# Routed experts of a two-layer decoder block: one written-out run of weight tiles, tokens gathered in float32r, gates applied at the add

## The reference

```python
def moe_swiglu(h, w_router, w_gate, w_up, w_down):
    probs = jax.nn.softmax((h @ w_router).astype(jnp.float32), axis=-1)
    top_p, top_i = lax.top_k(probs, TOP_K)                       # TOP_K = 2, N_EXPERTS = 8
    top_p = top_p / jnp.sum(top_p, axis=-1, keepdims=True)
    gates = jnp.sum(jax.nn.one_hot(top_i, N_EXPERTS, dtype=jnp.float32) * top_p[..., None], axis=-2)
    y = jnp.zeros(h.shape, jnp.float32)
    for e in range(N_EXPERTS):
        y = y + gates[..., e:e + 1] * swiglu(h, w_gate[e], w_up[e], w_down[e]).astype(jnp.float32)
    return y.astype(h.dtype)
```

## Time and profile before

| | us |
|---|---|
| median of 3 runs | 1809.09 (1803.16 to 1809.59) |
| the profiled execution | 1802.93 |
| its span | 1801.2 |
| around the span | 1.7 |
| first matmul of an expert tile starts | 766.32 |
| last matmul of an expert tile starts | 1781.75 |
| output DMA is issued | 1796.81 |

### The profile page before, as it was taken

The page is one execution under the profiler, slowest core; times in us unless marked ns, Lnnn a source line. Parts: engine busy times, 40 slices in busy tenths (PEclk is TensorE's granted clock), DMA queues, the critical chain, the costliest instruction groups (busy, mean ns, idle before and its releaser), DMA issues.

```text
span 1801.2 us, 28357 instructions
## 1 busy us (share of the span) xinstructions
PE 1729.2 (96%) x11390; PEld 1442.9 (80%) x11390; DVE 1274.9 (71%) x1185; ACT 966.4 (54%) x977; POOL 31.3 (2%) x93
## 2 busy tenths in 40 slices
PE   7999899999899999799999999999999999999997
PEld 5756899999677997478878788888788887788785
DVE  4671545542477655688888789888788897888885
ACT  2351534432143223276767667767667676667673
POOL 5000000000100000000000000000000000000000
PEclk9997999999999999899999999999999999999998
DMA  9210255453232004179999899999899998999992
GB/s 325 77 46 0 93 165 186 166 185 122 93 120 94 3 5 176 49 281 365 351 356 362 300 361 361 345 347 359 305 354 353 363 343 332 329 365 353 356 357 107
DMA packets 191227, 432.81 MB, mean 240 GB/s; under 512 B 9907, under 2 KB 10931, under 8 KB 191092
## 3 DMA queue, kind: packets, MB, share of 16 engines
q1 hardware_dynamic: 190704, 430.76, 66.0%
q10 hardware_dynamic: 388, 0.14, 0.0%
HBM read 429.82 MB, written 1.05 MB: 239 GB/s over the span
## 4 chain that ended last, share of the span: by engine, by line
PE 84%; DVE 9%; ACT 4%; issue 3%; ACTq 0%; DVEq 0%
PE ps L1012 16%; PE ps L1014 15%; PE ps L1013 15%; PE ps L667 5%; PE ps L665 5%; PE ps L666 5%; PE ps L584 2%; PE ps L714 2%; PE ps L979 2%; PE ps L994 2%; DVE wsplit L1783 2%; PE ps L656 2%; PE ps L934 2%; PE ps L833 1%; PE ps L848 1%
## 5 line engine op out<-in xcount | busy, mean ns | idle before, releaser
L1783 DVE TENSOR_TENSOR wsplit<-raw_w,wsplit 128x2048 fp32r<-128x2048 f32 x336 | 750.0, 2287 | 68.4 <-ACT wsplit L1347 68.4
L1347 ACT ACTIVATE wsplit<-raw_w 128x2048 fp32r<-128x2048 f32 x336 | 624.2, 1914 | 63.6 <-PE ps L1014 63.6
L1012 PE MATMUL ps<-wsplit,xsplit 128*128 128x512 f32 x896 | 360.4, 402 | 9.6 <-DVE wsplit L1783 8.1
L1014 PE MATMUL ps<-wsplit,xsplit 128*128 128x512 f32 x896 | 350.7, 391 | 0.0
L1013 PE MATMUL ps<-wsplit,xsplit 128*128 128x512 f32 x896 | 350.2, 391 | 0.0
L1012 PEld LDWEIGHTS ps<-wsplit,xsplit 128*128 128x128 f32 x896 | 169.0, 189 | 47.7 <-DVE wsplit L1783 12.7
L1014 PEld LDWEIGHTS ps<-wsplit,xsplit 128*128 128x128 f32 x896 | 169.0, 189 | 36.6
L1013 PEld LDWEIGHTS ps<-wsplit,xsplit 128*128 128x128 f32 x896 | 169.3, 189 | 36.2 <-issue 3.1
L1012 PE MATMUL ps<-wsplit,hsplit 128*128 128x512 f32 x448 | 179.6, 401 | 0.0
L1014 PE MATMUL ps<-wsplit,hsplit 128*128 128x512 f32 x448 | 174.6, 390 | 0.0
L1013 PE MATMUL ps<-wsplit,hsplit 128*128 128x512 f32 x448 | 174.5, 389 | 0.0
(11 more groups left out here) (320 smaller groups left out, 2258.0 us busy)
## 6 DMA issues: line engine op xcount, KB each, us to landing
raw_w<-in_moe_w_gate SPq DMA_DIRECT2D x114, 1024.0 KB, 6.5
raw_w<-in_moe_w_up SPq DMA_DIRECT2D x112, 1024.0 KB, 7.6
raw_w<-in_moe_w_down SPq DMA_DIRECT2D x112, 1024.0 KB, 7.0
ffn_raw<-in_ffn_w_gate SPq DMA_DIRECT2D x14, 1024.0 KB, 5.2
ffn_raw<-in_ffn_w_up SPq DMA_DIRECT2D x14, 1024.0 KB, 5.1
ffn_raw<-in_ffn_w_down SPq DMA_DIRECT2D x14, 1024.0 KB, 5.0
arena<-in_attn_w_qkv SPq DMA_DIRECT2D x3, 2048.0 KB, 13.0
arena<-in_attn_w_o SPq DMA_DIRECT2D x2, 2048.0 KB, 20.5
```

What stands on the lines that cost most here:

```text
L1012: mm(o, x_[0], w_[0], start=first_, stop=False)
L1014: return mm(o, x_[1], w_[0], start=False, stop=last_)
L1347: A(wsplit[:, m % NRING, 0, :], raw_w[:, m % NRAW, :], ACT.Copy).then_inc(w_hi, 1)
L1783: v.tensor_tensor(wsplit[:, m % NRING, 1, :], raw_w[:, m % NRAW, :], wsplit[:, m % NRING, 0, :].bitcast(F32), ALU.subtract).then_inc(w_lo, 1)
```

## The change

**No turns.** All eight experts are written out as one run of 56 blocks. The ring of weights runs through without a boundary. Loads, splits and tile matmuls are what they were. The pair of down tiles without an up tile between them comes once, at the very end.

**Gather.** The normed tokens `utok` are themselves split once into float32r high and low parts, the high one on ACT, the low one on POOL. `sel` of two experts is stored side by side, and one round r gathers 128 of the 1024 features for two experts: two matmuls of 256 columns for the high part and two for the low, in float32r. Two copies on one engine move the result to `xsplit` with nothing left to subtract. Eight rounds come ahead of the first tile, alternating between two PSUM banks and between ACT and DVE. For the other six experts the 3 x 8 rounds stand one by one between the tiles of blocks 3 to 5 of every odd expert, all on bank 5 and on ACT.

**Scatter.** `sel` itself, without gates, is transposed (`turn`). The result of an expert is split into `ye_hi` (ACT) and `ye_lo` (DVE), after the `lows` of the down tile, and a scatter is two float32r matmuls of 512 columns. The gate is multiplied in by DVE when it adds. The scatters of expert e-1 stand in blocks 1 and 2 of expert e; no scatter of zeros is left. At the end the four scatters use two banks, the last down half tile finishes one half of the result first, and the two `lows` for a second pass come after the adds.

The diff, cut to its core:

```diff
-        NB2 = 2 * FB
+        NB = EXPERTS * FB
...
-        TURNS = EXPERTS // 2
-        LATE = {0: (1, 0, 0), 1: (1, 2, 2), FB + 1: (0, 0, 4), FB + 2: (0, 2, 6)}
+        for e in range(EXPERTS):
+            USES[e * FB, 1] = ("turn", e, 0)
+            if e:
+                for o, (f, p) in enumerate(((1, 0), (1, 1), (2, 0), (2, 1))):
+                    USES[e * FB + f, p] = ("scatter", e - 1, o)
+            if e % 2 and e < EXPERTS - 1:
+                for r in range(KC):
+                    USES[e * FB + 3 + r // 3, r % 3] = ("gather", (e + 1) // 2, r)
...
@@ GpSimd @@
+            pool.wait_ge(utT_mm, 4)
+            for t in range(2):
+                pool.wait_ge(utok_hi_ok, t + 1)
+                g.tensor_tensor(utok_lo[:, t, :], utok[:, t, :], utok_hi[:, t, :].bitcast(F32), ALU.subtract).then_inc(utok_lo_ok, 1)
...
@@ TensorE @@
-                            last = mm(ps[:, 5 - half, q * P:(q + 1) * P], utok[:, t, k * P:(k + 1) * P],
-                                      sel[:, j, t, :], start=(t == 0), stop=(t == 1))
+                def gather(i, r, bank):
+                    if r == 0:
+                        pe.wait_ge(sel_ok, pas * 4 + (i + 1))
+                    for part, u_ in enumerate((utok_hi, utok_lo)):
+                        for t in range(2):
+                            last = mm(ps[:, bank, part * 2 * P:(part + 1) * 2 * P], u_[:, t, r * P:(r + 1) * P],
+                                      sel[:, t, :, :].rearrange("p j s -> p (j s)"), start=(t == 0), stop=(t == 1))
                     last.then_inc(xg_mm, 1)
...
+                def scatter(e, o, bank):
+                    n_, t = o // 2, o % 2
+                    if t == 0:
+                        pe.wait_ge(ye_lo_ok, pas * (2 * EXPERTS) + (2 * e + n_ + 2))
...
+                    mm(ps[:, bank, :], selT[:, e % 2, t, :], ye_hi[:, cs], start=True, stop=False)
+                    mm(ps[:, bank, :], selT[:, e % 2, t, :], ye_lo[:, cs], start=False, stop=True).then_inc(es_mm, 1)
...
+                for q in range(NB):
+                    gate_up(q, 0)
+                    between(q, 0)
+                    if q:
+                        hidden_tr(q - 1)
+                    gate_up(q, 1)
+                    between(q, 1)
+                    if q:
+                        down(q - 1)
+                        between(q, 2)
+                hidden_tr(NB - 1)
+                down(NB - 1)
...
@@ ScalarE @@
+                for n_, (kind, q) in enumerate(TILES):
+                    if kind == 0:
+                        made(n_)
...
+                        A(hbuf[:, q % 2, :], ps[:, q % 2, :], ACT.Silu).then_inc(e_silu, 1)
+                        between(q, 0)
+                        if q:
+                            hidden(q - 1)
+                    elif kind == 1:
+                        between(q, 1)
+                    elif q == NB - 1:
+                        hidden(q)
+                        result(EXPERTS - 1, n_)
+                    else:
+                        between(q + 1, 2)
+                    highs(*SPLITS[n_])
+                    if kind == 2 and q % FB == FB - 1 and q < NB - 1:
+                        result(q // FB, n_)
...
@@ VectorE @@
+                    v.scalar_tensor_tensor(a_, ps[:, bank, :], gate[:, t, e:e + 1], a_, ALU.mult, ALU.add).then_inc(es_add, 1)
...
+                    elif kind == 1:
...
+                        between(q, 1)
+                        if q % (2 * FB) == FB + 1 and q < NB - FB:
+                            choose(q // (2 * FB) + 1)
...
+                    if q < NB - 1 or kind < 2:
+                        lows(*SPLITS[n_])
+                    if kind == 2 and q % FB == FB - 1 and q < NB - 1:
+                        result_lo(q // FB)
                 for o in range(4):
-                    collect(o, turns * 8 + pas * 4 + (o + 1))
+                    collect(EXPERTS - 1, o, 5 - o % 2)
+                lows(*SPLITS[-1])
```

More of the change, by code:

```diff
@@ L969, in _ @@
             n = pe.value_load(npass_i[0:1, 0:1], min_val=1, max_val=2)
[L971 to L977 removed]
+            with pe.Fori(0, n) as pas:
+                def gather(i, r, bank):
+                    if r == 0:
+                        pe.wait_ge(sel_ok, pas * 4 + (i + 1))
+                    for part, u_ in enumerate((utok_hi, utok_lo)):
@@ new lines, in bank5_read, with between @@
+                def bank5_read(q, place):
+                    kind, e, o = LAST5[q, place]
+                    if kind == "gather":
+                        pe.wait_ge(xg_act, pas * XACT + (KC * e - KC // 2 + o + 1))
+                    elif kind == "turn":
+                        pe.wait_ge(st_ev, pas * EXPERTS + (e + 1))
+                    else:
+                        pe.wait_ge(es_add, pas * (4 * EXPERTS) + (4 * e + o + 2))
+                def between(q, place):
+                    if (q, place) in USES:
+                        kind, e, o = USES[q, place]
+                        bank5_read(q, place)
+                        if kind == "gather":
+                            gather(e, o, 5)
+                        elif kind == "turn":
+                            turn(e)
+                        else:
+                            scatter(e, o, 5)
@@ new lines, in _ @@
+                pe.wait_ge(utok_lo_ok, 2)
+                pe.wait_ge(es_add, pas * (4 * EXPERTS) + 1)
+                for r in range(KC):
+                    if r >= 2:
+                        pe.wait_ge((xg_act, xg_dve)[r % 2], pas * (XACT, XDVE)[r % 2] + (r // 2))
+                    gather(0, r, 5 - r % 2)
+                for q in range(NB):
[8 more added lines that the diff above has]
+                        between(q, 2)
@@ L1320, in _ @@
                 act.wait_ge(acc_ok, 2 * t + 2)
-                own.done(A(utok[:, t, :], acc[:, t, :], ACT.Square, accum_out=normcol[:, 2, t:t + 1]), n4_ss)
+                own.done(A(utok[:, t, :], acc[:, t, :], ACT.Square, accum_out=normcol[:, 2, t:t + 1]), act_own)
                 own.settle()
@@ L1332, in _ @@
                            ACT.Copy), utT_cp)
+            for t in range(2):
+                A(utok_hi[:, t, :], utok[:, t, :], ACT.Copy).then_inc(utok_hi_ok, 1)
             act.wait_ge(lg_sub, 1)
@@ L1768, in _ @@
             chosen, gate = route[:, 0, :, :], route[:, 10, :, :]
-            def choose(j, expert):
-                e = bass.ds(expert, 1)
-                for t in range(2):
-                    v.tensor_scalar(sel[:, j, t, :], slotno[:, :], ranks[:, t, e], chosen[:, t, e], ALU.is_equal, ALU.mult)
-                    last = v.tensor_scalar(selg[:, j, t, :], slotno[:, :], ranks[:, t, e], gate[:, t, e],
-                                           ALU.is_equal, ALU.mult)
-                last.then_inc(sel_ok, 1)
```

410 lines of the change are left out of this document (189 added, 221 removed).

## The result

The changed kernel takes 1763.8 us (median of 4 runs, 1760.8 to 1765.0) against 1806.1 (1802.9 to 1809.6) for the kernel before on the same chip, a ratio of 0.976 (95% interval 0.974 to 0.979). Forecast were 1768 and a range of 1750 to 1790. Its profiled execution took 1764.6 us, with a span of 1762.9; before it was 1802.9, so 38.3 us have gone in the profiles.

A forecast was written before the change was run, and what follows sets the result against it. PE was taken to set the pace. Gains of 45.1 us between tiles and 5.2 in the tail, less 12.2 and 1 at the start, net 37: 1766 profiled, 1768 as median, range 1750 to 1790.

The forecast's parts named there:

- Scatters: Between tiles, 32 float32 scatters of 0.87 us become 28 of two float32r matmuls of 0.227: gain 15.0 us.
- Gathers: Between tiles, 8 gathers of 3.65 us become 24 rounds of 0.48: gain 17.7 us.
- The rival of 256 columns at float32's pace: Gather matmuls of 256 columns in float32r run no faster than float32: 1801 to 1803 us, no change; 5%.
- Turn ends: Three PE waits of 3.1 us, laid to DVE's `lows` behind `gate_rows`, go: gain 8.4; clock and issue time 4 more.
- The wait for ye_lo: PE waits 1.3 us for DVE's low part before the first scatter, at seven experts: loss 9.1 us.
- The clock at each expert (rival): The seven waits each bring a stretch at clock 0.50, costing 1.6 us: 11 more, 1779 us; 12%.
- ACT in the gather rounds: Copies ahead of `hidden` or `highs` fit by 0.5 us at place 0, 0.3 at places 1 and 2: no loss.
- small waits: Rival: the gather rounds' slack of 0.3 to 0.5 us fails, 24 x 0.5 = 12 us, 1780; 10%.
- the slower one: Rival: ACT is late by its queue place, all 24 gather rounds losing 1.9 us: 1814 us; 6%.
- DMA (rival): Weights can't come faster than before, 347 GB/s, so only the tail is won: 1798 us; 7%.
- The tail: From the last tile's end to the output DMA's issue, 14.8 us become 9.6: gain 5.2.
- The start: Ahead of the first tile, gather rounds win nothing; POOL beside DVE's routing chain adds 1 us for contention.

## Why the prediction was right, step by step

**Scatters: right.** 28 at 0.45 in the distances between tiles, as forecast; putting them back to float32 gave 0.87 again.

**Gathers: right.** 24 rounds at 0.48, and leaving them out gave 11.7 in the run of tiles. The rival of 256 columns at float32's pace is out.

**Turn ends: the sum right, the reason half right.** Forecast 12.4 with the clock; the run of tiles lost 12.3 when both causes were taken out of the kernel before. The step that failed is "because DVE's `lows` stand behind `gate_rows`": with only that mended the run of tiles is 2.7 us longer and the whole time the same. The 0.95 us of the earlier trace rows, which the prediction took as all there is to PE's own return, was only the end of it that stuck out behind DVE's wait. In the clear the returns cost 12.0 us. The change took both away, so the error didn't show in its time: that this term came out is luck as far as its reason goes. On a kernel that had only reordered DVE it would have been 12 us of gain promised and none had.

**The wait for ye_lo: right in place, a little large.** Seven waits of 1.03 to 1.08 (forecast 1.3), 7.4 instead of 9.1, and moving `ye_lo` won 7.5.

**The clock at each expert (rival): out.** The granted clock is 1.00 through the seven waits.

**choose: 0.3 each instead of 0.5.** Three waits, 0.9 us; the end of the run 1.75 (forecast 1.6).

**ACT in the gather rounds: right that it costs nothing, the slack mis-sized.** The prediction had 0.5 at place 0 and 0.3 at places 1 and 2. Measured are 0.84 behind place 0, a little under 0.53 behind the last round of an expert and over 1.06 behind the others: 0.53 us more per round cost 0.8 us in all, 1.06 more cost 4.7. The chain counted two copies as 0.76 where they hold ACT for 0.54, since they overlap; `highs` start 1.21 us behind the first gather record (967.41 to 968.62), not 1.44. At places 1 and 2 it also left out that between the tile's end and the need for the low stand two rounds and one tile, not one of each (0.48 more), except behind the last round. So the rival "small waits" and the slower one needed three times the copies to cost anything clear, and then 0.37 us in nine rounds. The slower rival's sum has a slip besides: 24 x 1.9 is 46 us, so 1812 and not 1814.

**DMA (rival): out.** 353 GB/s over the whole run, and no wait for a load.

**The tail: right.** 9.3 us, forecast 9.6.

**The start: the loss of 1 us did not come.** In the profiled execution the first tile came 5.0 us later than in the earlier trace rows (771.36 against 766.32), and that is why 37.8 + 5.5 of gain made 38.3. 4.0 us of it was there already when the router's matmuls began (747.70 against 743.68), in code that isn't changed. The start moves as much between kernels in which nothing ahead of the experts is changed: the three with edits at the turn ends had their first tile at 765.3, 770.0 and 772.6. In the router's matmuls 1.7 us more were spent (granted clock 0.51 from 747 to 768). What the change does touch comes behind them: from the last router matmul to the first tile are 17.1 us in the changed kernel (16.9 to 17.3 in six of its variants), 17.8 before and 17.4 to 18.6 in the three variants of the kernel before. So 0.7 us were won there in the profiles. POOL's subtractions cost nothing, since the chain began as they ended; with POOL beside the whole chain the same distance is 20.1, so work of POOL in that place costs some 3 us.

**Sum.** Forecast net 37.0, of it 32.9 in the run of tiles, 5.2 in the tail and 1 lost at the start. Measured in the two profiles: 37.8, 5.5 and 5.0 lost, of which 5.7 lie ahead of what the change touches. The run of tiles is 4.9 better than forecast: 1.7 at `ye_lo`, 0.6 at `choose`, and for the rest eight stalls of 0.32 us between tiles (2.6 in all), which stand in the distances of starts before and not after, which the prediction hadn't counted and whose cause no row names. Against the forecast the start is 4.0 worse and the run of tiles 4.9 better. The two nearly cancel in the profiled executions, so the closeness of 1764.6 to the forecast's 1766 is in part luck.

## What to carry to other kernels

Where the profile puts a wait down to one engine, another delay of the same length may end just ahead of it. Before a gain is promised for the one, take it away in the code as it is and see what the engine waits for then. A loop's return is such a delay, and here writing out the one engine that sets the pace was enough, with the other delay mended too. And a split that makes PE's part cheaper needs its low part in time: put the small subtraction between two large ones in DVE's queue, not behind them, or the gain goes to the wait.

## What the runs showed of the hardware

With `gate_rows` moved, PE's return to the start of a loop of about 250 us came as two stretches of "issue": 2.39 and 2.33 us at turn 1, up to 3.18 at turn 3. The second did not lie at the start of the loop but six tile matmuls later, and that is the place of the 0.95 us of the earlier trace rows too. Both went when PE's loop was written out.

The clock did not follow the length of the idle time simply. Seven idle stretches of 0.8 us in the changed kernel left it at 1.00, and so did 2.39, 2.33 and 2.89 us in the kernel with `gate_rows` moved. At the end of turn 3 there it was 0.50 from 1540.0 to 1543.4, and so had fallen 0.6 us before the idle stretch of 3.18 us ended (1540.63). 2.71 us before were followed by 0.50 at turn 2, and by 1.00 at turn 1 (the line below, its columns as above); with PE's loop written out the same 2.71 us were followed by 0.50 at all three ends, at the third only 1.5 us after PE had begun again (1529.16, and 0.50 from 1530.7). The kernel before:

```profile
1018.90:1022.00 3.10, 1.67 (x6) 1.23 (x7) 3.10 (x3) 3.09 (x3) 0.00 (x0) 1.00 0.28 55
```

A small two-input operation of DVE that began inside a GpSimd instruction of 0.9 us ended 0.03 us behind it, eight times of eight, and so took 0.05 to 0.59 us longer; reductions beside the same instructions took their usual 0.17.
